# The experts' second product turned around: v stationary, the tokens' weights moving, the sum kept as features by tokens

## The chip, the cores and the metric

One Trainium2 chip, one NeuronCore of it. The metric is the device time of one execution of the whole program in microseconds (us). Everything is float32 at the inputs and the output; inside, most matrix products run on pairs of rounded float32 values (type fp32r), a high part and a rest, so that one exact product is three matmuls.

## The reference, cut to what matters

The program is two transformer blocks one behind the other on 256 tokens of 1024 features. The change touches only the last step of each of the two layers of the second block, a feed-forward part with 16,384 experts of which every token takes 128:

```
q = xn @ wq;  scores against 2 x 128 subkeys;  top 16 x 16;  idx, g = 128 experts and gates of each token
act = gelu(einsum('ckd,cd->ck', u_tab[idx], xn))
out = einsum('ck,ckd->cd', g * act, v_tab[idx])          # c token, k picked expert, d feature
x = x + out
```

The kernel doesn't gather the picked experts. It computes the product of every token with every expert's row of u (16,384 x 1024), multiplies it by a gate that is zero where the expert was not picked, and multiplies that with the whole of v (16,384 x 1024). The second of these products, weights (256 tokens x 16,384) times v, is what the change turns around.

## The kernel before, in words

The state x lives in SBUF as hT, features on the partitions (8 chunks of 128), tokens along the free dimension. The experts are worked off in 128 tiles t of 128 experts each (class Experts). A tile of u or v is one transfer of 512 KB. It lands in one of four slots of a ring (raw), is taken as two halves of 128 x 512, and each half is rounded by ScalarE into w_hi (line 214), while VectorE makes the rest w_lo (line 223). TensorE takes a half when its w_lo is made, and frees it with the last matmul that reads it; ScalarE may then round a later half into the same buffer. Four such buffers are in turn.

For the first 33 tiles (EARLY) the products with u were done ahead, so that the loop over t begins with 33 rounds that hold nothing but the product with v. In the other 95 tiles each round holds, on TensorE's queue, first the product of tile t + 1 with u (function product, lines 608 to 610: a 128 x 128 piece of the ring is stationary, 256 tokens move, 24 matmuls), and then the product of tile t with v (function add_up, lines 2088 to 2090). Beside that runs a chain between the two: ScalarE takes the gelu of the product out of PSUM (line 2103), VectorE multiplies by the gates (2130), ScalarE rounds the result (wt_hi, 2119), and VectorE makes its rest (wt_lo, 2146). It has a whole round of time.

In add_up the weights of 128 tokens are stationary and a half of v, 512 columns, moves: two groups of tokens, two halves, three matmuls each, so 12 matmuls of 512 columns, into four PSUM banks (acc) that sum over all 128 tiles, tokens on the partitions. At the end of a layer that sum stands the wrong way round for hT. So the four banks are copied to SBUF (VectorE line 2136, ScalarE 2109), turned by 16 TensorE transposes in eight groups (line 2074) into two PSUM banks in turn, and VectorE adds each group of features to hT (line 2140, eight times). The last of these additions releases the next layer, or the transfer of the output.

All queues are written in the order in which their engine executes them; nothing reorders the program.

Of the kernel before, what the change touches and what calls it, by code (L numbers as in the profile page):

```python
# [10 lines left out]
ACT = mybir.ActivationFunctionType  # L11
ALU = mybir.AluOpType
AX = mybir.AxisListType

P = 128
D = 1024
DC = D // P
LAT = 256
CTX = 256
# [12 lines left out]
NKEY = 128  # L32
# [16 lines left out]
class Span:  # L49


    def __init__(self, sem, first):
        self.sem, self.first = sem, first
# [112 lines left out]
def flat(ap):  # L166
    return ap.rearrange("p a b -> p (a b)")
# [1858 lines left out]
class Experts:  # L2026


    def __init__(self, k, l, x_hi, x_lo, early, gates, start):
        self.k, self.l, self.x_hi, self.x_lo, self.early, self.gates = k, l, x_hi, x_lo, early, gates  # L2030
        self.start = start
        self.ge = k.sb("ge", [P, 2, LAT], 151040)
        self.wt_hi = k.sb("wt_hi", [P, 2, LAT], 153088, F32R)
        self.wt_lo = k.sb("wt_lo", [P, 2, LAT], 155136, F32R)
        self.scores = {t: k.bank[t % 2].use(written=0) for t in range(EARLY, NKEY)}
        self.acc = [k.bank[2 + n].use(written=0) for n in range(4)]
        self.gated = k.named("scores_gated").take(NKEY - EARLY)
        self.hi = k.named("weights_t_rounded").take(NKEY)
        self.lo = k.named("weights_t_rest").take(NKEY)
        self.rowbuf = flat(gates[:, 0:8, :])  # L2040
        self.turns = [k.bank[n % 2].use() for n in range(DC)]
        self.done = [u.emptied() for u in self.turns[-2:]]

    def load(self, kind, t):
        self.k.ring.load(self.k.io[f"{kind}{self.l}"][t], (kind, self.l, t))
# [13 lines left out]
    def tensor(self):  # L2059
        k, pe = self.k, self.k.nc.tensor  # L2060
        for t in range(NKEY):
            if EARLY <= t + 1 < NKEY:
                use = self.scores[t + 1]
                pe.wait_ge(*use.free())
                product(k, use.tensor, [DC], lambda c: (self.x_hi[:, c, :], self.x_lo[:, c, :]), LAT)
            self.add_up(t)
        for n in range(DC):
            use = self.turns[n]
            if n == 0:
                for a in self.acc:  # L2070
                    pe.wait_ge(*a.emptied())
            pe.wait_ge(*use.free())
            for tt in range(2):
                m = pe.transpose(use.tensor[:, tt * P:(tt + 1) * P], self.rowbuf[:, tt * D + n * P:tt * D + (n + 1) * P],
                                 k.ident)
            m.then_inc(use.written.sem, 1)

    def add_up(self, t):
        k, pe, s = self.k, self.k.nc.tensor, t % 2
        pe.wait_ge(*self.lo.after(t + 1))  # L2080
        if t == 0:
            for a in self.acc:
                pe.wait_ge(*a.free())
        for half in range(2):
            hi, lo = k.ring.take()
            for tt in range(2):
                rows, out = slice(tt * P, (tt + 1) * P), self.acc[2 * tt + half].tensor[:]
                pe.matmul(out, self.wt_hi[:, s, rows], hi, start=(t == 0), stop=False, skip_group_check=True)  # L2088
                pe.matmul(out, self.wt_hi[:, s, rows], lo, start=False, stop=False, skip_group_check=True)  # L2089
                m = pe.matmul(out, self.wt_lo[:, s, rows], hi, start=False, stop=(t == NKEY - 1),  # L2090
                              skip_group_check=True)
            k.ring.free(m)

    def scalar(self):
        k, act = self.k, self.k.nc.scalar
        hold(act, self.start)
        self.round_weights(0)
        for t in range(NKEY):
            if EARLY <= t + 1 < NKEY:
                k.ring.round(2)  # L2100
                use = self.scores[t + 1]
                act.wait_ge(*k.ring.freed_of(("u", self.l, t + 1)))
                act.activation(self.ge[:, (t + 1) % 2, :], use.tensor[:, 0:LAT], ACT.Gelu).then_inc(use.read.sem, 1)
            if t + 1 < NKEY:
                self.round_weights(t + 1)
            k.ring.round(2)
        act.wait_ge(*k.ring.freed_of(("v", self.l, NKEY - 1)))
        for n in (1, 3):
            act.activation(self.rowbuf[:, n * 512:(n + 1) * 512], self.acc[n].tensor[:],
                           ACT.Copy).then_inc(self.acc[n].read.sem, 1)  # L2110

    def round_weights(self, t):
        act, s = self.k.nc.scalar, t % 2
# [7 lines left out]
    def vector(self):  # L2121
        k, dve = self.k, self.k.nc.vector
# [9 lines left out]
                self.weights_rest(t + 1)  # L2132
            k.ring.remain(2)
        dve.wait_ge(*k.ring.freed_of(("v", self.l, NKEY - 1)))
        for n in (0, 2):
            dve.tensor_copy(self.rowbuf[:, n * 512:(n + 1) * 512], self.acc[n].tensor[:]).then_inc(self.acc[n].read.sem, 1)
        for n, use in enumerate(self.turns):
            x = k.hT[:, n, CTX:]
            dve.wait_ge(*use.full())
            dve.tensor_tensor(x, x, use.tensor[:, 0:LAT], ALU.add).then_inc(use.read.sem, 1)  # L2140

    def weights_rest(self, t):
        dve, s = self.k.nc.vector, t % 2
# [301 lines left out]
```

## Time and profile before

| | us |
|---|---|
| Runs shown, median (lowest to highest of 3) | 3836.66 (3831.36 to 11778.27) |
| The profiled execution, its own time | 3843.8 |
| Its span in the profile | 3842.5 |
| Mean granted TensorE clock, share of 2.4 GHz | 0.923 |
| The experts' stage of the first layer, first to last matmul with v | 1986.5 to 2620.7 |
| The same of the second layer | 3199.0 to 3832.0 |
| From there to the issue of the output's transfer | 3832.0 to 3837.7 |

One of the three runs took 11778.27 us, far from the others; the median is not moved by it. Of the page, the busy line says how much of the span an engine had an instruction in progress, and the chain of waits says which instructions the end of the program depended on. For TensorE two rows of instructions are listed: PE, the matmuls, and PEld, the loads of the stationary operand. Their listed durations reach from issue to the drained result and overlap each other. What a matmul costs in a stream is the distance from its start to the next one's start, and that is what the rows below are for.

### The profile page before, as it was taken

How to read it: one execution, taken by the hardware profiler on the slowest of the kernel's cores; microseconds unless marked ns; L12 is line 12 of the kernel's file. 1: busy time of each engine (PE TensorE's matmuls, PEld its weight loads, DVE VectorE, ACT ScalarE, POOL GpSimd, SP SyncE). 2: the span in 40 equal slices, each digit the busy share in tenths (PEclk: the TensorE clock that was granted, in tenths of full speed). 3: DMA queues.
4: the chain of work that ended last, by engine and by line, in shares of the span. 5: the costliest groups of instructions: out<-in, count | busy, mean ns of one | idle time of the engine just before them, and what ended most of it. 6: DMA issues, size and time to landing. Idle time of an engine off the chain costs nothing.

```text
span 3842.5 us, 51118 instructions
## 1 busy us (share of the span) xinstructions
PE 3449.5 (90%) x19132; PEld 2853.0 (74%) x19132; DVE 2288.9 (60%) x4729; ACT 1810.7 (47%) x3796; POOL 0.2 (0%) x4
## 2 busy tenths in 40 slices
PE   7899889999979989589779999998869968999999
PEld 2474447887748988388668999997659857899998
DVE  6633334333465645768876666665665986666665
ACT  6622333332344534252585555554334196555554
POOL 0000000000000000000000000000000000000000
PEclk9897888999889989589999999998769999999999
DMA  8820001223203543044115555553204403555554
GB/s 310 286 99 11 1 23 66 99 90 94 94 5 110 179 139 122 0 138 143 66 53 184 186 187 187 186 186 128 72 26 161 160 1 125 186 186 186 186 186 154
DMA packets 134925, 479.90 MB, mean 125 GB/s; under 512 B 15384, under 2 KB 17304, under 8 KB 133912
## 3 DMA queue, kind: packets, MB, share of 16 engines
q1 hardware_dynamic: 130352, 463.53, 36.1%
q10 hardware_dynamic: 4328, 13.11, 0.9%
q8 instruction: 154, 2.52, 0.3%
q14 instruction: 91, 0.75, 0.1%
HBM read 475.53 MB, written 1.05 MB: 124 GB/s over the span
## 4 chain that ended last, share of the span: by engine, by line
PE 83%; DVE 9%; issue 3%; DMA 3%; ACT 3%; ACTq 0%; DVEq 0%
PE bank L608 14%; PE bank L610 13%; PE bank L609 13%; PE bank L2089 6%; PE bank L2088 6%; PE bank L2090 6%; PE bank L2014 6%; PE bank L1938 4%; PE bank L475 3%; PE bank L882 3%; DMA raw<-in_mod_w 2%; DVE conv L1313 1%; PE bank L484 1%; PE bank L892 1%; PE bank L1119 1%
## 5 line engine op out<-in xcount | busy, mean ns | idle before, releaser
L223 DVE TENSOR_TENSOR w_lo<-raw,w_hi 128x512 fp32r<-128x512 f32 x1664 | 1124.5, 691 | 798.3 <-ACT w_hi L214 769.0
L214 ACT ACTIVATE w_hi<-raw 128x512 fp32r<-128x512 f32 x1664 | 1011.9, 626 | 814.3 <-PE bank L610 606.6
L608 PE MATMUL bank<-x_hi,w_hi 128*128 128x256 f32 x2096 | 597.5, 285 | 14.9 <-DVE w_lo L223 7.3
L609 PE MATMUL bank<-x_lo,w_hi 128*128 128x256 f32 x2096 | 595.5, 284 | 0.0
L610 PE MATMUL bank<-x_hi,w_lo 128*128 128x256 f32 x2096 | 593.4, 283 | 0.0
L608 PEld LDWEIGHTS bank<-x_hi,w_hi 128*128 128x128 f32 x2096 | 398.1, 190 | 26.4 <-issue 8.2
L2088 PE MATMUL bank<-w_hi,wt_hi 128*128 128x512 f32 x1024 | 406.2, 397 | 6.5 <-DVE wt_lo L2146 6.5
L2089 PE MATMUL bank<-w_lo,wt_hi 128*128 128x512 f32 x1024 | 407.5, 398 | 0.0
L2090 PE MATMUL bank<-w_hi,wt_lo 128*128 128x512 f32 x1024 | 405.8, 396 | 0.0
L609 PEld LDWEIGHTS bank<-x_lo,w_hi 128*128 128x128 f32 x2096 | 398.2, 190 | 8.0
L610 PEld LDWEIGHTS bank<-x_hi,w_lo 128*128 128x128 f32 x2096 | 399.9, 191 | 0.0
L608 PE MATMUL bank<-a_hi,w_hi 128*128 128x512 f32 (+1 forms) x880 | 309.1, 351 | 18.0 <-DVE a_lo L580 18.0
L610 PE MATMUL bank<-a_hi,w_lo 128*128 128x512 f32 (+1 forms) x880 | 303.9, 345 | 0.0
L609 PE MATMUL bank<-a_lo,w_hi 128*128 128x512 f32 (+1 forms) x880 | 302.0, 343 | 0.0
L2014 PE MATMUL bank<-xn,u_raw 128*128 128x256 f32 x1056 | 228.2, 379 | 0.0
L2088 PEld LDWEIGHTS bank<-w_hi,wt_hi 128*128 128x128 f32 x1024 | 193.5, 189 | 45.9 <-DVE wt_lo L2146 6.9
L2090 PEld LDWEIGHTS bank<-w_hi,wt_lo 128*128 128x128 f32 x1024 | 193.2, 189 | 46.2
L1938 PE MATMUL bank<-hT,first 128*128 128x128 f32 x1024 | 147.5, 289 | 83.1 <-issue 77.2
L2089 PEld LDWEIGHTS bank<-w_lo,wt_hi 128*128 128x128 f32 x1024 | 193.8, 189 | 38.0
L2014 PEld LDWEIGHTS bank<-xn,u_raw 128*128 128x128 f32 x1056 | 200.5, 190 | 27.2
L1938 PEld LDWEIGHTS bank<-hT,first 128*128 128x128 f32 x1024 | 127.0, 195 | 103.7 <-issue 97.4
L608 PEld LDWEIGHTS bank<-a_hi,w_hi 128*128 128x128 f32 x880 | 167.6, 190 | 47.3 <-issue 13.9
(318 smaller groups left out, 4947.5 us busy)
## 6 DMA issues: line engine op xcount, KB each, us to landing
raw<-in_v SPq DMA_DIRECT2D x256, 512.0 KB, 4.4
raw<-in_u SPq DMA_DIRECT2D x190, 512.0 KB, 3.5
raw<-in_mod_w SPq DMA_DIRECT2D x96, 512.0 KB, 4.8
raw<-in_w_gate_up SPq DMA_DIRECT2D x88, 512.0 KB, 3.5
u_raw<-in_u SPq DMA_DIRECT2D x66, 512.0 KB, 3.5
raw<-in_w_in SPq DMA_DIRECT2D x40, 512.0 KB, 4.0
raw<-in_w_down SPq DMA_DIRECT2D x32, 512.0 KB, 3.5
raw<-in_w_peer SPq DMA_DIRECT2D x32, 512.0 KB, 3.9
```

Of the source, the lines that this page charges most:

```text
L214: self.nc.scalar.activation(self.hi[:, m % 4, :], self.half(m), ACT.Copy).then_inc(self.rounded[m % 4], 1)
L223: self.nc.vector.tensor_tensor(self.lo[:, m % 4, :], self.half(m), self.hi[:, m % 4, :], ALU.subtract).then_inc(self.ready[m % 4], 1)
L475: m = pe.matmul(self.sums.tensor[:, 4 * at:4 * at + P // group], k.sq[:, n % 4, t * P:(t + 1) * P], indicators[group], start=(n == 0 and t ...
L608: pe.matmul(out[:, 0:width], hi[:, w], x_hi, start=(c == 0), stop=False)
L609: pe.matmul(out[:, 0:width], hi[:, w], x_lo, start=False, stop=False)
L610: mm = pe.matmul(out[:, 0:width], lo[:, w], x_hi, start=False, stop=(c == total - 1))
L882: m = pe.matmul(use.tensor[:, 0:self.keys[r]], l, x, start=(j == 0), stop=(j == len(pairs) - 1))
L1938: m = pe.matmul(use.tensor[:, t * P:(t + 1) * P], self.first[:, g % 4, t, :], self.rows(g, t), start=True, stop=True)
L2014: m = pe.matmul(use.tensor[:, 0:LAT], self.raw[:, t % 3, c * P:(c + 1) * P], self.xn[:, c, :], start=(c == 0), stop=(c == DC - 1))
L2088: pe.matmul(out, self.wt_hi[:, s, rows], hi, start=(t == 0), stop=False, skip_group_check=True)
L2089: pe.matmul(out, self.wt_hi[:, s, rows], lo, start=False, stop=False, skip_group_check=True)
L2090: m = pe.matmul(out, self.wt_lo[:, s, rows], hi, start=False, stop=(t == NKEY - 1), skip_group_check=True)
```

## The change

The product with v is written the other way round. A 128 x 128 piece of the ring's half of v is stationary, and all 256 tokens' weights of the tile move. There are eight such pieces in a tile (four in each half) and three matmuls for each, so 24 matmuls of 256 columns take the place of 12 of 512. Each writes half a PSUM bank; the same four banks hold the sum, now features on the partitions and tokens along the free dimension, two chunks of features in a bank. The sum then stands as hT does: the copies to SBUF and the transposes are gone, and VectorE adds each bank to two chunks of hT in one instruction.

```
-        self.rowbuf = flat(gates[:, 0:8, :])
-        self.turns = [k.bank[n % 2].use() for n in range(DC)]
-        self.done = [u.emptied() for u in self.turns[-2:]]
+        self.done = [a.emptied() for a in self.acc]
...
             self.add_up(t)
-        for n in range(DC):
-            use = self.turns[n]
-            if n == 0:
-                for a in self.acc:
-                    pe.wait_ge(*a.emptied())
-            pe.wait_ge(*use.free())
-            for tt in range(2):
-                m = pe.transpose(use.tensor[:, tt * P:(tt + 1) * P], self.rowbuf[:, tt * D + n * P:tt * D + (n + 1) * P],
-                                 k.ident)
-            m.then_inc(use.written.sem, 1)
...
+        last = t == NKEY - 1
         for half in range(2):
             hi, lo = k.ring.take()
-            for tt in range(2):
-                rows, out = slice(tt * P, (tt + 1) * P), self.acc[2 * tt + half].tensor[:]
-                pe.matmul(out, self.wt_hi[:, s, rows], hi, start=(t == 0), stop=False, skip_group_check=True)
-                pe.matmul(out, self.wt_hi[:, s, rows], lo, start=False, stop=False, skip_group_check=True)
-                m = pe.matmul(out, self.wt_lo[:, s, rows], hi, start=False, stop=(t == NKEY - 1),
-                              skip_group_check=True)
+            for j in range(4):
+                c, cols = 4 * half + j, slice(j * P, (j + 1) * P)
+                out = self.acc[c // 2].tensor[:, (c % 2) * LAT:(c % 2 + 1) * LAT]
+                pe.matmul(out, hi[:, cols], self.wt_hi[:, s, :], start=(t == 0 and c % 2 == 0), stop=False,
+                          skip_group_check=True)
+                pe.matmul(out, hi[:, cols], self.wt_lo[:, s, :], start=False, stop=False, skip_group_check=True)
+                m = pe.matmul(out, lo[:, cols], self.wt_hi[:, s, :], start=False, stop=last, skip_group_check=True)
             k.ring.free(m)
...
-        act.wait_ge(*k.ring.freed_of(("v", self.l, NKEY - 1)))
-        for n in (1, 3):
-            act.activation(self.rowbuf[:, n * 512:(n + 1) * 512], self.acc[n].tensor[:],
-                           ACT.Copy).then_inc(self.acc[n].read.sem, 1)
...
         dve.wait_ge(*k.ring.freed_of(("v", self.l, NKEY - 1)))
-        for n in (0, 2):
-            dve.tensor_copy(self.rowbuf[:, n * 512:(n + 1) * 512], self.acc[n].tensor[:]).then_inc(self.acc[n].read.sem, 1)
-        for n, use in enumerate(self.turns):
-            x = k.hT[:, n, CTX:]
-            dve.wait_ge(*use.full())
-            dve.tensor_tensor(x, x, use.tensor[:, 0:LAT], ALU.add).then_inc(use.read.sem, 1)
+        for n, use in enumerate(self.acc):
+            x = k.hT[:, 2 * n:2 * n + 2, CTX:]
+            dve.tensor_tensor(x, x, use.tensor[:].rearrange("p (c t) -> p c t", c=2), ALU.add).then_inc(use.read.sem, 1)
```

The instructions move as follows. TensorE's queue at the end of the first layer's experts, before the change, ends with the sum, then the transposes, then the next layer's first norm (in these names wt is the tokens' weights, w the ring, and the number at a name counts the program's buffers):

```order
L2088 MATMUL bank<-w_hi_51,wt_hi_165 128x512
L2089 MATMUL bank<-w_lo_52,wt_hi_165 128x512
L2090 MATMUL bank<-w_hi_51,wt_lo_166 128x512
L2074 MATMUL bank<-cmat_54,gates_145 128x128 x16
L475 MATMUL bank<-ones_53,sq_57 128x1 x32
L484 MATMUL bank<-cmat_54,spread_58 128x128 x4
```

With the change the same place reads:

```order
L2078 MATMUL bank<-wt_hi_165,w_hi_51 128x256
L2080 MATMUL bank<-wt_lo_166,w_hi_51 128x256
L2081 MATMUL bank<-wt_hi_165,w_lo_52 128x256
L475 MATMUL bank<-ones_53,sq_57 128x1 x32
L484 MATMUL bank<-cmat_54,spread_58 128x128 x4
```

Three matmuls of 512 columns stood for a quarter of a tile, and now three of 256 stand for an eighth. The line of the 16 transposes is gone, and the next layer's norm follows the sum directly. VectorE's queue at the end of the program, as a difference:

```order
 L223 TENSOR_TENSOR w_lo_52<-raw_50,w_hi_51 128x512
-L2136 COPY gates_198<-bank 128x512 x2
-L2140 TENSOR_TENSOR hT_49<-hT_49,bank 128x256 x8
+L2123 TENSOR_TENSOR hT_49<-hT_49,bank 128x2x256 x4
```

Two copies and eight additions of 256 columns were there; four additions of 512 columns are there now, and nothing of TensorE stands between them. The transfers on SyncE's queue are the same, in the same order.

## Rows read from the trace of the kernel before

**Rows 1.** The page's busy line: busy us, share of the span, instructions.
```profile
PE 3449.5 (90%) x19132; PEld 2853.0 (74%) x19132; DVE 2288.9 (60%) x4729; ACT 1810.7 (47%) x3796; POOL 0.2 (0%) x4
```

**Rows 2.** The page's chain of waits, by line, as shares of the span.
```profile
PE bank L608 14%; PE bank L610 13%; PE bank L609 13%; PE bank L2089 6%; PE bank L2088 6%; PE bank L2090 6%; PE bank L2014 6%; PE bank L1938 4%; PE bank L475 3%; PE bank L882 3%; DMA raw<-in_mod_w 2%; DVE conv L1313 1%; PE bank L484 1%; PE bank L892 1%; PE bank L1119 1%
```

**Rows 3.** Busy times, clock and transfers of five stretches (us from the span's start).
```profile
core 0: us, PE busy (x) PEld busy (x) DVE busy (x) ACT busy (x) POOL busy (x), PEclk, DMA share, GB/s
1700.00:1740.00 40.00, 40.00 (x336) 40.00 (x335) 19.93 (x31) 20.94 (x40) 0.00 (x0) 1.00 0.64 218
1995.00:2075.00 80.00, 80.00 (x343) 64.34 (x342) 51.49 (x86) 44.67 (x85) 0.00 (x0) 1.00 0.55 187
2100.00:2600.00 500.00, 500.00 (x3171) 452.08 (x3170) 310.76 (x530) 274.22 (x530) 0.00 (x0) 1.00 0.56 186
2653.00:2656.00 3.00, 2.86 (x12) 2.81 (x12) 3.00 (x9) 1.76 (x5) 0.00 (x0) 0.50 0.03 5
2657.00:2661.00 4.00, 2.97 (x21) 2.36 (x19) 4.00 (x13) 2.40 (x6) 0.00 (x0) 1.00 0.00 0
```

**Rows 4.** Timeline of one round: start, us, engine, line; product with v begins at 2302.53.
```profile
2302.53 0.39 PE L2088 MATMUL bank<-w_hi,wt_hi 128*128 128x512 f32 x1
2302.54 0.19 PEld L2089 LDWEIGHTS bank<-w_lo,wt_hi 128*128 128x128 f32 x1
2302.76 0.40 PE L2089 MATMUL bank<-w_lo,wt_hi 128*128 128x512 f32 x1
2303.00 0.39 PE L2090 MATMUL bank<-w_hi,wt_lo 128*128 128x512 f32 x1
...
2305.33 0.28 PE L608 MATMUL bank<-x_hi,w_hi 128*128 128x256 f32 x1
2305.34 0.19 PEld L609 LDWEIGHTS bank<-x_lo,w_hi 128*128 128x128 f32 x1
2305.45 0.28 PE L609 MATMUL bank<-x_lo,w_hi 128*128 128x256 f32 x1
2305.57 0.28 PE L610 MATMUL bank<-x_hi,w_lo 128*128 128x256 f32 x1
...
2308.22 0.39 PE L2088 MATMUL bank<-w_hi,wt_hi 128*128 128x512 f32 x1
```

**Rows 5.** One line's instructions in all the program: the loads before L609's matmuls.
```profile
L609 PEld LDWEIGHTS bank<-x_lo,w_hi x2096: 187/188/338, 1441.4 to 3825.8; 128*128 128x128 f32 x191
```

**Rows 6.** The chain of waits in order of time, at the early products with u.
```profile
1749.64 113.98 PE bank L2014 x528
```

**Rows 7.** Timeline of the last end: from the last matmul to the output's transfer.
```profile
3831.57 0.39 PE L2090 MATMUL bank<-w_hi,wt_lo 128*128 128x512 f32 x1
3831.99 1.29 DVE L2136 COPY gates<-bank 128x512 f32<-128x512 f32 x2 [3.07 <-PE bank L2090]
3833.50 0.63 PE L2074 MATMUL bank<-cmat,gates 128*128 128x128 f32 x4 [1.54 <-DVE gates L2136]
...
3836.80 0.75 DVE L2140 TENSOR_TENSOR hT<-hT,bank 128x256 f32<-128x256 f32 x2 [0.20 <-PE bank L2074]
3837.65 0.63 SPq L2255 DMA_DIRECT2D out<-hT  x1
```

**Rows 8.** By line, shapes apart: a VectorE operation on 512 columns of PSUM and SBUF.
```profile
L1417 DVE TENSOR_TENSOR hid<-gate,bank 128x512 f32<-128x512 f32 x22 | 15.2, 689 | 30.5 <-PE bank L610 30.5
```

**Rows 9.** Timeline behind the first layer's end: copies, last additions, the next layer's start.
```profile
2620.74 1.29 DVE L2136 COPY gates<-bank 128x512 f32<-128x512 f32 x2
...
2625.55 0.75 DVE L2140 TENSOR_TENSOR hT<-hT,bank 128x256 f32<-128x256 f32 x2 [0.20 <-PE bank L2074]
2626.39 0.33 ACTq L256 DMA_DIRECT2D memT<-in_memT  x1
...
2634.61 13.79 PE L475 MATMUL bank<-ones,sq 128*128 128x1 f32 x64 [8.76 <-ACT sq L435]
```

**Rows 10.** Timeline of the ring in that round: ScalarE rounds, VectorE makes the rest.
```profile
2303.93 1.14 ACT L214 ACTIVATE w_hi<-raw 128x512 fp32r<-128x512 f32 x2
2304.06 0.42 DVE L2146 TENSOR_TENSOR wt_lo<-ge,wt_hi 128x256 fp32r<-128x256 f32 x1 [0.49 <-ACT wt_hi L2119]
2304.59 1.29 DVE L223 TENSOR_TENSOR w_lo<-raw,w_hi 128x512 fp32r<-128x512 f32 x2
2305.59 0.63 ACT L214 ACTIVATE w_hi<-raw 128x512 fp32r<-128x512 f32 x1 [0.52 <-PE bank L2090]
2306.26 0.69 DVE L223 TENSOR_TENSOR w_lo<-raw,w_hi 128x512 fp32r<-128x512 f32 x1 [0.38 <-ACT w_hi L214]
```

## The prediction

> **What bounds the kernel now.** I read the page's busy line first. TensorE has a matmul in progress for 90% of the span and no other engine comes near [rows 1]. That alone proves little, as such durations overlap, so the chain of waits comes next: the lines of the two expert products and their likes (608 to 610, 2088 to 2090) are most of it [rows 2]. Lines 2088 to 2090 are 18% of the span, some 690 us, and these are what the change rewrites. Then I asked for the experts' stage as stretches. In the part with both products, the stretch from 2100 to 2600, TensorE is busy for 500.00 of 500 us at a granted clock of 1.00 (the level of 2.4 GHz), VectorE for 311, ScalarE for 274, the transfers for 56% [rows 3]. In the part with v alone, from 1995 to 2075, it is 80.00 of 80 us [rows 3]. So the stage is paced by TensorE's stream without a gap, and a nanosecond more or less per matmul reaches the end in full. What a matmul costs is then the distance of starts in the timeline [rows 4].
>
> **The stream.** Removed: 12 matmuls of 512 columns in each of 128 tiles and two layers, 3,072. Added: 24 of 256 columns, 6,144. The columns are the same, 6,144 a tile. The old price: from 2302.53 to 2305.33 twelve matmuls take 2.80 us, 0.2333 each [rows 4]; in the part with v alone a window of 80 us holds 343 records, one or two of them begun before it, so 0.234 each, 2.81 us for twelve [rows 3]. The new price stands in the same round: lines 608 to 610 have exactly the new form, a piece of the ring stationary, 256 columns of tokens moving, three matmuls for a piece, and from 2305.33 to 2308.22 the 24 of them take 2.89 us [rows 4]. Over the 500 us the mean comes out a hair lower: 3,168 starts are 88 rounds of 5.68 us, less 2.80 is 2.88, 0.120 each. I take 2.88. Then each of the 95 rounds with both products costs 0.08 us more, each of the 33 with v alone 0.07, in two layers: 190 x 0.08 + 66 x 0.07 = **+19.8 us**.
>
> Each of the new matmuls brings its load of the stationary operand, so that 12 more loads a tile are to be hidden. A load is listed with 188 ns [rows 5], longer than the 120 ns between matmuls, yet the load for line 609 begins at 2305.34, just behind the start of line 608's matmul, and line 609's matmul follows at 2305.45 [rows 4]. Loads run beside the matmuls and beside each other. Until now the 512-column matmuls left them slack (452 of 500 us busy). A stretch without any is 1700 to 1740, the projection of the queries: loads busy 40.00 of 40 us and 336 matmuls, 0.120 each [rows 3]. A full load side therefore doesn't slow the stream beyond the 0.120 that I charge.
>
> Here a rule can be weighed. Between the price of a 512 and of two 256 the rows show 2 x 0.120 - 0.2333 = 6.7 ns. The Trainium skill (TensorE: Matmul & The Clock Gate, Back-to-back issue gap) gives the distance as columns over 2.4 GHz plus about 2.5 ns, so splitting a matmul costs 2.5 ns: its stream term would be +7.7 us in place of +19.8, the time 3838, which is counted with the first of the rivals. Its 216 ns for 512 columns is not what these rows show (233), so I take the rows.
>
> **The ring.** A half is consumed in 1.44 us where it was 1.40, and freed by its last matmul as before. ScalarE's rounding and VectorE's rest take 0.63 and 0.69 [rows 10], and each engine is idle for over a third of the stage [rows 3], so both keep up, more easily than before since the round is longer. The transfers (186 GB/s) have also more time. The gelu chain ends, with wt_lo at 2304.48 [rows 10], before the round's product with u even begins at 2305.33, and is needed at 2308.22: 3.7 us of slack. None of these costs or gains anything. While the clock is granted at 0.50 the columns cost twice as much either way; a split of equal columns changes nothing there.
>
> **The end of a layer.** Before: copies at 3831.99, the last pair of additions done at 3836.80 + 0.75 = 3837.55, 5.56 us [rows 7]; in the first layer 2620.74 to 2626.30, 5.56 as well [rows 9]. Now four additions of 512 columns follow the last matmul. The row nearest to them is a VectorE operation on 512 columns of PSUM and SBUF, 689 ns [rows 8]; two in a row take 1.29, not 1.38 [rows 7], so four take 0.69 + 3 x 0.60 = 2.5 to 4 x 0.69 = 2.8 us. With 2.6, each layer saves 3.0: **-6 us**. Nothing covers this tail: in the first layer ScalarE's transfers for the next mixer wait for it and are issued at 2626.39, and the next matmul comes 8.76 us after the last transpose [rows 9]; all that moves up. ScalarE's two copies were beside VectorE's and give nothing of their own. Without the transposes TensorE idles 11 to 12 us there instead of 8.8. It is at half clock anyway when it resumes and stays there: 2653 to 2656 has 0.50, 2657 to 2661 1.00 [rows 3]. The moment at which full clock returns may shift against the work by some us, which is worth at most 2 us here and at the like places behind it; I keep that as +-4 in the range and zero in the sum.
>
> **The sum.** +19.8 - 6.0 = +14 us. The profiled execution's own 3843.8 becomes 3858. It lies 7 us above the median of the runs shown; against that median, 3836.7, the forecast is **3851 us**, 0.4% slower. About 2% (77 us) is what a measurement of this kernel can tell from no change, so the forecast is "the same".
>
> **The rivals.**
>
> *The split is free.* If a moving operand that ScalarE and VectorE are just writing (the ring) is what makes 512 columns cost 0.2333, the old form paid for it and the new one, whose moving operand is quiet, does not. For it: line 2014, plain matmuls that move xn, takes 113.98 / 528 = 0.216 [rows 6] for the same 256 tokens in its type, less than 0.2333 for twice 256. Against it: line 608 moves quiet x as well and still pays 0.120. With 2 x 0.1167 the sum is -6: 3831. With 0.108 for each, half of line 2014's, it is 24 x 0.108 = 2.59 a tile, -0.21 x 256 - 6 = -60: 3777, 1.6% faster. Chances: 0.09 for the first, 0.03 for the second. That the queue keeps a stationary piece for two matmuls and drops a load would land here too; line 609 reuses line 608's piece today and has 2,096 loads of its own [rows 5].
>
> *The loads come out from behind the matmuls.* Place: add_up, where until now 512-column matmuls let the load side run ahead; with rounds of 48 short ones it can't. If the stream fell to one load at a time, 188 ns [rows 5], it would be 6,144 x (0.188 - 0.1167) = +438 us, 4270; it decides from 0.1167 + 77 / 6,144 = 0.129 us a matmul on, where the time is 2% up. Against it stands the stretch with the loads busy 40.00 of 40 us at 0.120 [rows 3]. The Trainium skill (the same page, The mechanism, in the part on packing small matmuls) says that a load overlaps a matmul in flight only when it goes to other rows of the array, which these full loads never do. By that rule nothing would overlap and this rival would hold; the trace disagrees, 0.11 to 0.12 us between starts with loads of 0.19 [rows 4]. Chance 0.03.
>
> *A little of it.* The new stream differs from line 608's in that it goes round four banks in half-bank pieces and that there is no other kind of matmul between. If it costs 0.123 to 0.129 that is +18 to +55 on the forecast, 3869 to 3906. Nothing in the rows asks for it. Chance 0.05.
>
> **How the numbers follow.** The forecast has the remaining 0.80. Its own spread: 1.5 ns on the price of a new matmul is 9 us, the clock 4, the tails 1, and two executions shown differ by 12; together about 3836 to 3868. The range takes in the free split at 3831 and the foot of the last rival: 3832 to 3871. Faster by over 2% would need more than the second free case: 0.01. Slower by over 2%: the loads and the far end of the last rival, 0.05. Within: 0.94.
>
> **What would show it.** Right: lines 2078 to 2081 with 6,144 matmuls of 256 columns; rounds of 5.76 us in the part with both products and 2.88 in the part with v alone; PEld busy near 100% of a stretch of 500 us; the experts' stages about 10 us longer each; from the last matmul to the output's issue 2.7 us instead of 5.7. Wrong: a distance of starts in add_up under 0.118 or over 0.123, a gap of TensorE behind line 223, or DVE and ACT suddenly waiting for something other than TensorE. What would overturn it most simply is a price of a moving column that depends on which buffer moves.

## The result and the profile after

The changed kernel takes 3849.43 us (median of 11 runs, 3845.79 to 3855.45), the kernel before 3836.11 (11 runs). The ratio is 1.0036 with a 95% interval of 1.0027 to 1.0044: 13.8 us slower, 10 to 17 by the interval. That is clear of noise and far inside 2%. (A difference with an interval is here, and below, the ratio of the runs times the time of the kernel before; the two medians alone differ by 13.3.) The forecast was 3851 and +14.

The two profiled executions differ by less, 3848.3 - 3842.5 = 5.8 us of span, and it takes the traces to see why. They can be laid side by side at four marks: the first and last matmul with v in each layer's experts' stage. These rows are from the timeline of the kernel before (start, us, engine, line; its last mark stands in [rows 7]):

```profile
1986.53 0.50 PE L2088 MATMUL bank<-w_hi,wt_hi 128*128 128x512 f32 x1 [3.27 <-DVE wt_lo L2146]
...
2620.31 0.40 PE L2090 MATMUL bank<-w_hi,wt_lo 128*128 128x512 f32 x1
...
3198.40 0.50 PE L2088 MATMUL bank<-w_hi,wt_hi 128*128 128x512 f32 x1 [3.27 <-DVE wt_lo L2146]
```

And these are from that of the changed kernel:

```profile
1977.66 0.58 PE L2078 MATMUL bank<-wt_hi,w_hi 128*128 128x256 f32 x1 [3.27 <-DVE wt_lo L2129]
...
2622.07 0.27 PE L2081 MATMUL bank<-wt_hi,w_lo 128*128 128x256 f32 x1
2622.38 2.48 DVE L2123 TENSOR_TENSOR hT<-hT,bank 128x512 f32<-128x512 f32 x4
2624.97 0.33 ACTq L256 DMA_DIRECT2D memT<-in_memT  x1
...
3196.86 0.38 PE L2078 MATMUL bank<-wt_hi,w_hi 128*128 128x256 f32 x1 [3.27 <-DVE wt_lo L2129]
...
3840.57 0.28 PE L2081 MATMUL bank<-wt_hi,w_lo 128*128 128x256 f32 x1
3840.89 2.48 DVE L2123 TENSOR_TENSOR hT<-hT,bank 128x512 f32<-128x512 f32 x4 [3.22 <-PE bank L2081]
3843.47 0.63 SPq L2238 DMA_DIRECT2D out<-hT  x1
```

| From start to start of the marks, us | before | after | difference |
|---|---|---|---|
| Start to the first stage (code that is not changed) | 1986.53 | 1977.66 | -8.9 |
| First stage | 633.8 | 644.4 | +10.6 |
| To the second stage, with the first layer's end | 578.1 | 574.8 | -3.3 |
| Second stage | 633.2 | 643.7 | +10.5 |
| Last matmul to the output's issue | 6.08 | 2.90 | -3.2 |

(The second stage of before begins with a matmul at 3198.40; the 3199.0 of the table ahead is half a microsecond late, and its other late marks are the ends of the last matmuls, 0.4 us behind their starts.) So in this pair of profiles the change costs 21.2 us in the stream and gives back 6.5 at the two ends. The 8.9 us in the first row lie in code that both kernels share, and hide more than half of it in this pair of profiles. Most of them arise around the first attention, where the one execution was granted its full clock earlier. One stretch of before and the same of after, columns as in [rows 3] (the second kernel is 2 us further on in its work where the stretch begins):

```profile
345.00:372.00 27.00, 27.00 (x56) 12.00 (x55) 7.82 (x20) 9.21 (x24) 0.00 (x0) 0.54 0.00 1
```

```profile
345.00:372.00 27.00, 26.91 (x80) 12.48 (x80) 10.51 (x28) 12.48 (x35) 0.00 (x0) 0.89 0.00 1
```

At a mean granted clock of 0.54 TensorE gets through 56 records, at 0.89 through 80, in code that is the same. In eleven profiles of this work the first stage begins between 1969.9 and 1986.5 us, the kernel before being the latest of all. A pair of profiles cannot weigh 14 us in this kernel; stage lengths can, they repeat within 1.2 us for one stream.

The stream itself, in the stretches that answer to [rows 3] (v alone, then both products):

```profile
1995.00:2075.00 80.00, 80.00 (x669) 80.00 (x669) 50.15 (x83) 43.23 (x82) 0.00 (x0) 1.00 0.54 184
2100.00:2600.00 500.00, 500.00 (x4169) 500.00 (x4169) 306.81 (x521) 269.77 (x521) 0.00 (x0) 1.00 0.56 183
```

TensorE is busy throughout as before, and now its loads are too, 500.00 of 500 us where they were 452. One or two records were begun before the window, so 4,167 matmuls in 500 us are 0.1200 each, and a round of 48 is 5.76 us. In the timeline the order is as regular as line 608's was; the second column is again each one's own duration, the distance of starts is the price:

```profile
2305.15 0.29 PE L609 MATMUL bank<-x_lo,w_hi 128*128 128x256 f32 x1
2305.27 0.28 PE L610 MATMUL bank<-x_hi,w_lo 128*128 128x256 f32 x1
2305.39 0.28 PE L2078 MATMUL bank<-wt_hi,w_hi 128*128 128x256 f32 x1
2305.51 0.28 PE L2080 MATMUL bank<-wt_lo,w_hi 128*128 128x256 f32 x1
2305.63 0.28 PE L2081 MATMUL bank<-wt_hi,w_lo 128*128 128x256 f32 x1
...
2308.27 0.28 PE L608 MATMUL bank<-x_hi,w_hi 128*128 128x256 f32 x1
```

From 2305.39 to 2308.27, 24 matmuls take 2.88 us; the twelve of before took 2.80 [rows 4].

### The profile page after: what moved, and what is told of

Its sections match the earlier page's. It is cut to its first block, busy times and chain, and to the rows that moved or that the text cites. A ratio compares the mean times of both kernels' runs of the same rounds, so it can differ in the third digit from the quotient of the medians.

```text
span 3848.3 us, 57182 instructions
## 1 busy us (share of the span) xinstructions
PE 3455.4 (90%) x22172; PEld 3007.1 (78%) x22172; DVE 2284.3 (59%) x4717; ACT 1807.5 (47%) x3792; POOL 0.2 (0%) x4
## 4 chain that ended last, share of the span: by engine, by line
PE 82%; DVE 9%; issue 3%; DMA 3%; ACT 3%; ACTq 0%; DVEq 0%
PE bank L608 14%; PE bank L609 13%; PE bank L610 13%; PE bank L2078 6%; PE bank L2080 6%; PE bank L2081 6%; PE bank L2014 6%; PE bank L1938 4%; PE bank L475 3%; DMA raw<-in_mod_w 2%; PE bank L882 2%; DVE conv L1313 1%; PE bank L484 1%; PE bank L892 1%; DVE stats L931 1%
## 5 line engine op out<-in xcount | busy, mean ns | idle before, releaser
L608 PE MATMUL bank<-x_hi,w_hi 128*128 128x256 f32 x2096 | 598.0, 285 | 14.8 <-DVE w_lo L223 7.3
L609 PE MATMUL bank<-x_lo,w_hi 128*128 128x256 f32 x2096 | 596.3, 284 | 0.0
L2078 PE MATMUL bank<-wt_hi,w_hi 128*128 128x256 f32 x2048 | 578.7, 283 | 6.5 <-DVE wt_lo L2129 6.5
L2080 PE MATMUL bank<-wt_lo,w_hi 128*128 128x256 f32 x2048 | 580.8, 284 | 0.0
L2081 PE MATMUL bank<-wt_hi,w_lo 128*128 128x256 f32 x2048 | 578.1, 282 | 0.0
L609 PEld LDWEIGHTS bank<-x_lo,w_hi 128*128 128x128 f32 x2096 | 398.6, 190 | 0.0
L2078 PEld LDWEIGHTS bank<-wt_hi,w_hi 128*128 128x128 f32 x2048 | 387.8, 189 | 6.9 <-DVE wt_lo L2129 6.9
L2081 PEld LDWEIGHTS bank<-wt_hi,w_lo 128*128 128x128 f32 x2048 | 389.1, 190 | 0.0
L2080 PEld LDWEIGHTS bank<-wt_lo,w_hi 128*128 128x128 f32 x2048 | 385.5, 188 | 0.0
L609 PE MATMUL bank<-a_lo,w_hi 128*128 128x512 f32 (+1 forms) x880 | 305.9, 348 | 0.0
```

Source lines behind the costliest of these rows:

```text
L608: pe.matmul(out[:, 0:width], hi[:, w], x_hi, start=(c == 0), stop=False)
L609: pe.matmul(out[:, 0:width], hi[:, w], x_lo, start=False, stop=False)
L2078: pe.matmul(out, hi[:, cols], self.wt_hi[:, s, :], start=(t == 0 and c % 2 == 0), stop=False, skip_group_check=True)
L2080: pe.matmul(out, hi[:, cols], self.wt_lo[:, s, :], start=False, stop=False, skip_group_check=True)
L2081: m = pe.matmul(out, lo[:, cols], self.wt_hi[:, s, :], start=False, stop=last, skip_group_check=True)
```

## The experiments

Nine kernels, to take the sum apart and then to price a matmul by itself.

### The split alone

```
-                pe.matmul(out, self.wt_hi[:, s, rows], hi, start=(t == 0), stop=False, skip_group_check=True)
+                for x in range(2):
+                    n = slice(x * 256, (x + 1) * 256)
+                    pe.matmul(out[:, n], self.wt_hi[:, s, rows], hi[:, n], start=(t == 0 and x == 0), stop=False,
+                              skip_group_check=True)
```

(and the two matmuls behind it in the same way.)

> The kernel before with its 512-column matmuls of the v product each cut in two of 256 columns: the weights stay stationary, the ring still moves, the old end of a layer stays. It is the stream half of the change alone, without turning the operands. My theory (a matmul of 256 columns of these pairs has one price, about 0.120 us, whichever operand moves, and two of them cost 6 to 7 ns more than one of 512): the distance of starts in the v product is 0.120, each experts' stage 10.6 us longer than 633.5, 3836 + 21 = 3857 us in all. Rival (the moving ring, which is being written, costs extra per column, and the change escaped a part of that): the distance is clearly above 0.120, 0.123 or more, 3875 us or more. Rival (a repeated stationary operand makes its second load cheap): under 0.118, 3845 us or less.

Measured: 3846.29 us, ratio 1.0024 (1.0013 to 1.0035) to the kernel before, which took 3834.76 beside these runs: +9.2 us with 5 to 13 by the interval. The two stages are 639.5 and 640.2 us, 12.8 more than before in all. Both are under my 21. The distance of starts in the v product is 0.1188, under my 0.120 and over the 0.118 of the rival with the cheap second load, so neither theory has it:

```profile
2100.00:2600.00 500.00, 500.00 (x4194) 500.00 (x4192) 308.06 (x523) 271.57 (x524) 0.00 (x0) 1.00 0.57 185
```

4,194 records against the changed kernel's 4,169, with the same 48 matmuls a round, and the half of these that are lines 608 to 610 lie at 0.120 in both. So splitting costs 2 x 0.1188 - 0.2335 = 4 ns a pair, about 13 us, and turning the operands another 1.2 ns a matmul, 7.4 us. By the stages turning costs 8.4 us (1288.1 against 1279.7); the last microsecond lies in lines 608 to 610, 0.2 ns each.

### The end of a layer alone

```
-        for n in (0, 2):
-            dve.tensor_copy(self.rowbuf[:, n * 512:(n + 1) * 512], self.acc[n].tensor[:]).then_inc(self.acc[n].read.sem, 1)
-        for n, use in enumerate(self.turns):
...
+        for n, use in enumerate(self.acc):
+            x = k.hT[:, 2 * n:2 * n + 2, CTX:]
+            dve.tensor_tensor(x, x, use.tensor[:].rearrange("p (c t) -> p c t", c=2), ALU.add).then_inc(use.read.sem, 1)
```

> The kernel before with only the end of a layer changed: the copies and transposes are left out and the four accumulators, which still hold tokens by features, are added to the state as they stand, so the values are not the reference's. It is the other half of the change alone. My theory: from the start of the last matmul to the output's issue 2.9 us in place of 6.1, 3.2 us less at each of two layers, 3836 - 6.4 = 3830 us. Rival (the next layer's start is held by something else, such as its transfers or the clock's return, so that only the last layer gains): 3833 us. If both halves are additive, this one and the split sum up to the changed kernel's +13 us.

Measured: 3829.79 us, ratio 0.998 (0.9967 to 0.9993), 7.7 us less, 3 to 13 by the interval. The stages stay (1267.1 us in all, before 1266.9). The timeline's end:

```profile
3830.33 0.39 PE L2078 MATMUL bank<-w_hi,wt_lo 128*128 128x512 f32 x1
3830.76 2.48 DVE L2121 TENSOR_TENSOR hT<-hT,bank 128x512 f32<-128x512 f32 x4 [3.07 <-PE bank L2078]
3833.33 0.63 SPq L2236 DMA_DIRECT2D out<-hT  x1
```

3.00 us from the last matmul to the output's issue, 6.08 before; 3.1 less. The first layer's end is as short here and in the changed kernel, where it is 2622.07 to 2624.97, 2.90 us. But the rival (only the last layer gains, for the clock's return) is not refuted: its 3833 lies inside the interval, and in this very profile the second stage begins 578.7 us after the end of the first, not earlier than before (578.1). The next mixer does start earlier; what it gained is lost within 130 us of the first stage's end. These are the same 652 matmuls, from the mixer's first one of line 608 on, in the kernel before, the changed kernel and this one:

```profile
2653.90:2750.20 96.30, 87.18 (x652) 85.39 (x651) 52.18 (x99) 45.24 (x92) 0.00 (x0) 0.91 0.37 122
```

```profile
2652.30:2748.60 96.30, 87.18 (x652) 85.44 (x652) 52.23 (x99) 45.25 (x92) 0.00 (x0) 0.91 0.38 122
```

```profile
2649.90:2749.00 99.10, 90.71 (x652) 89.32 (x652) 52.24 (x99) 45.25 (x92) 0.00 (x0) 0.86 0.38 118
```

At a mean granted clock of 0.86 instead of 0.91 they take 2.8 us more. Of the eight profiles with the short end, four have 574.8 to 576.2 us between the stages and four 577.9 to 578.7; the two with the old end have 578.1 and 578.5. So the last layer's 3.1 us reach the end in each of them, the first layer's only where the clock doesn't take them back. Averaged over runs more than the one end comes through: the changed kernel is 13.8 us slower (10 to 17) with 21.2 us in its stages, which leaves 7.4 (4 to 11) for the ends. With both ends in full the halves add up: 12.8 + 8.4 - 6.4 = +14.8, measured +13.8.

### Turned, but 512 columns wide

```
+            twice = [wt[:, s, :].unsqueeze(1).to_broadcast([P, 2, LAT]) for wt in (self.wt_hi, self.wt_lo)]
+            for j in range(2):
+                cols = slice(2 * j * P, (2 * j + 1) * P)
+                out = self.acc[2 * half + j].tensor[:].rearrange("p (c t) -> p c t", c=2)
+                pe.matmul(out, hi[:, cols], twice[0], start=(t == 0), stop=False, skip_group_check=True)
```

> The changed kernel, but with only every second piece of v as the stationary operand (half the features are left out) and the tokens' weights moving twice in one matmul of 512 columns: 12 matmuls of 512 columns a tile, with the operands in the new places. Same columns as before and after. My theory (the price goes by the width alone): the distance of starts is 0.2335 as before the change, the stages 633.5 us, the end of a layer short: 3836 - 6.4 = 3830 us. Rival (a quiet moving operand streams faster than the ring): 0.216 to 0.230, that is 3775 to 3820 us.

Measured: 3832.52 us, ratio 0.9989 (0.9976 to 1.0002). The stages are 633.4 and 634.1 us, 1267.5 in all, and the stretch has the counts of [rows 3] to the record:

```profile
2100.00:2600.00 500.00, 500.00 (x3171) 451.81 (x3171) 310.88 (x529) 273.63 (x528) 0.00 (x0) 1.00 0.59 186
```

At 512 columns it makes no difference whether the ring or the weights move: 0.2335 either way. The rival of the quiet operand falls. What the change lost it lost by the width, and in the 256-column form alone the turned placing costs something too. (Between the stages this profile has 578.0 us, one of the four in which the first end's gain is lost again; by the runs it is 4 us less than before, 9 less to 1 more, where I expected 6.4 less.)

### The prices with nothing else running

```
+        for _ in range(96):
+            pe.matmul(out[:, 0:512], wt[:, 0:128], hi, start=True, stop=True)
+        for _ in range(96):
+            pe.matmul(out[:, 0:384], wt[:, 0:128], hi[:, 0:384], start=True, stop=True)
+        for _ in range(96):
+            pe.matmul(out[:, 0:256], wt[:, 0:128], hi[:, 0:256], start=True, stop=True)
+        for _ in range(96):
+            pe.matmul(out[:, 0:256], hi[:, 0:128], wt, start=True, stop=True)
...
```

> The changed kernel with eight segments of 96 matmuls of the same pairs behind the last layer, when ScalarE, VectorE and the ring's transfers stand still: 512, 384 and 256 columns with the weights' buffer stationary (128 wide); 256 with the ring's piece stationary; the last with a stationary operand of 64 columns, and 512 with one of 64; then 96 in the exact order and banks of the changed product and 96 in the order of the old one cut in two. They write sums that are read by nobody. Theory A (the pair type itself costs 0.444 ns a column plus a fixed 6 ns): at full clock 0.2335, 0.177 and 0.1195 to 0.120 even when nothing else runs, and 64-wide loads change nothing. Theory B (the 8% over 0.4167 ns a column is the traffic of ScalarE, VectorE and the transfers): 0.216, 0.163 and 0.109. Theory C (the load of 128 columns is what makes 256 columns cost 0.119 instead of 0.117): the 64-wide segment of 256 columns is at 0.117 or less while the 512 ones are alike. For the 1.2 ns between the turned order (120.0) and the cut old order (118.85): if it comes from the operands themselves, the last two segments show it too; if from the ring being rewritten, they are equal.

The chain of waits in order of time merges each segment: start, us, count. The first runs partly at half clock.

```profile
3850.19 24.05 PE bank L2260 x96
3874.24 16.65 PE bank L2262 x96
3890.89 11.39 PE bank L2264 x96
3902.28 11.51 PE bank L2266 x96
3913.80 11.23 PE bank L2268 x96
3925.02 21.78 PE bank L2270 x96
```

Divided: 384 columns 0.1734; 256 with the weights stationary 0.1186; 256 turned 0.1199; 256 turned with 64-wide loads 0.1170; 512 with 64-wide loads 0.2269. The full-clock part of the first is 0.2343 each. The last two segments, in the order of the changed product and of the split one, come to 0.1200 and 0.1187. Theory B falls clearly: with VectorE, ScalarE and the transfers silent every price is what it was in the stage. The 1.2 ns of turning are there as well (1.3 here), so they are not the ring being rewritten. Theory A holds for 512 and 256, misses 384 by 4 ns (0.177 expected), and was wrong on the loads: a 64-wide one makes 256 columns 3 ns cheaper, as theory C has it, but also 512 columns by 7 ns, where theory C expected no change and where the load side is idle for 40% of the time (11.33 of 19 us busy from 3926 to 3945). A 64-wide stationary piece also writes 64 partitions of the sum instead of 128; no run tells that from the shorter load.

### Half-wide loads in the real stream

```
-                c, cols = 4 * half + j, slice(j * P, (j + 1) * P)
+                c, cols = 4 * half + j, slice(j * P, j * P + 64)
```

> The changed kernel with 64 of the 128 columns of each stationary piece (half of the features are left out), so that each load is half as long while the 24 matmuls of 256 columns a tile stay. Theory A (the price of a matmul is its columns plus a fixed part, loads are hidden in full): 0.120 as before, experts' stages 644 us, 3849 us. Theory C (the load side, busy for 500 of 500 us, holds the stream back a little): the distance falls to 0.117 or less in the v product while lines 608 to 610 stay at 0.120, the stages 635 us or shorter, 3830 us.

Measured: 3827.32 us in one run, stages 638.6 and 633.5 us, against 644.4 and 643.7. The distance in the v product fell to 0.1183 in the first layer and to 0.1167 in the second, while lines 608 to 610 stayed at 0.120. Two stretches, one of each layer:

```profile
2100.00:2600.00 500.00, 500.00 (x4198) 500.00 (x4197) 308.82 (x526) 272.12 (x526) 0.00 (x0) 1.00 0.57 185
3300.00:3800.00 500.00, 500.00 (x4228) 500.00 (x4227) 311.00 (x529) 273.61 (x528) 0.00 (x0) 1.00 0.58 186
```

Theory C is right in direction, and in the second layer in size: a stationary piece of half the width makes the stream of 256 columns a little faster. That it is the load that holds it back is argued, not shown, for the reason given above. Why the same code runs at two prices in two layers stays open.

### The three matmuls in another order

```
-                pe.matmul(out, hi[:, cols], self.wt_lo[:, s, :], start=False, stop=False, skip_group_check=True)
-                m = pe.matmul(out, lo[:, cols], self.wt_hi[:, s, :], start=False, stop=last, skip_group_check=True)
+                pe.matmul(out, lo[:, cols], self.wt_hi[:, s, :], start=False, stop=False, skip_group_check=True)
+                m = pe.matmul(out, hi[:, cols], self.wt_lo[:, s, :], start=False, stop=last, skip_group_check=True)
```

> The changed kernel with the second and third matmul of each piece exchanged: high part times high weights, rest times high weights, high part times rest of the weights. Now the moving operand repeats behind itself where the stationary one did. If the 1.2 ns by which the turned product lies over the cut old one (118.85) depends on a stationary operand repeating, the distance changes (below 119.5 or above 120.5, the stage by 4 us or more); if it depends on which buffer is stationary, it stays 120.0 and the stage 644 us.

Measured: 3850.54 us in one run, both stages 643.7, and the same 4,169 matmuls in the stretch as in the changed kernel:

```profile
2100.00:2600.00 500.00, 500.00 (x4169) 500.00 (x4168) 306.70 (x521) 270.12 (x521) 0.00 (x0) 1.00 0.56 183
```

A repeated stationary operand brings nothing and costs nothing.

### Which buffer is stationary, which moves

Thirteen segments as in the quiet experiment, all 256 columns and 128-wide loads, and three of other widths:

```
+        for _ in range(64):
+            m = pe.matmul(out[:, 0:256], x[:, 0:128], hi[:, 0:256], start=True, stop=True)
+        for _ in range(64):
+            m = pe.matmul(out[:, 0:256], hi[:, 0:128], x[:, 0:256], start=True, stop=True)
...
```

> The changed kernel with sixteen segments of 64 matmuls behind the last layer, nothing else running: 256 columns with a 128-wide stationary operand in thirteen pairs of buffers (weights, rest of weights, two ring buffers, the ring's rest, two chunks of x), then a stationary operand of 32 columns with 256, then 512 and 320 columns. They write sums that nobody reads. Theory A (which buffer is stationary and which moves has its own price, by where the two lie in SBUF): weights stationary and ring moving 118.7 ns, the turned pair 120.0, and other pairs fall on these two or more levels by their places. Theory B (it is not the place, and the 1.3 ns between the segments before was their order in time): all thirteen within 0.4 ns. For the load: 32 columns stationary at 116.9 as 64 were if 116.7 is the floor of the moving side, lower if the load still counts. Widths: 320 at 0.148 to 0.149 and 512 at 0.233 if a fixed part of 6 ns stands beside 0.444 ns a column.

Four rows of the chain: weights stationary and ring moving, the turned pair, x stationary and ring moving, 320 columns.

```profile
3851.35 7.51 PE bank L2263 x64
3858.86 7.68 PE bank L2265 x64
3897.25 7.59 PE bank L2275 x64
3973.36 9.39 PE bank L2293 x64
```

0.1173, 0.1200, 0.1186 and 0.1467. Ten of the thirteen pairs lie at 0.120; only the three whose moving operand is the ring's buffer and whose stationary one is not come out lower, at 0.1173 to 0.1187. That looks like theory A, but the pair of weights and ring, 0.1186 in the quiet experiment, is 0.1173 here with the same instructions, so the place is not all of it. What makes the 1 to 3 ns is not settled. With a 32-wide load the same pair took 0.1178, no less than its 0.1173 with a 128-wide one: here a load of a quarter of the width brought nothing, which speaks against the load as the cause of these 1 to 3 ns.

### Where loads become the bound

```
+        for _ in range(80):
+            m = pe.matmul(out[0:128, 0:128], hi[:, 0:128], wh[:, 0:128], start=True, stop=True)
...
+        for _ in range(80):
+            m = pe.matmul(out[0:64, 0:128], hi[:, 0:64], wh[:, 0:128], start=True, stop=True)
...
```

> The changed kernel with ten segments of 80 matmuls of the pair type behind the last layer, nothing else running, the ring's buffer stationary and the weights' moving as in the changed product: 256, 224, 192, 128 and 64 moving columns with 128 stationary; 256, 224, 128 and 64 with 64 stationary; 256 with 96 stationary. Theory C (the 120 ns of the changed product lie just over a floor that loads of 128 columns set, so the split had used up nearly all that hides them): the distance stops falling soon under 256 columns, at 107 to 118 ns, and falls on only with 64 stationary. Theory A (loads are hidden with much to spare, the 2 to 3 ns are a small fixed cost): it falls in step with the columns, 105 at 224, 91 at 192, 62 at 128, alike for both widths. A third outcome: columns cost more under 256, so that the short ones are no cheaper than 120, with either width.

Again the chain, one row a segment: 256, 224, 192, 128 and 64 columns on 128-wide loads, 256, 224, 128 and 64 on 64-wide ones, 256 on a 96-wide one.

```profile
3856.64 9.60 PE bank L2263 x80
3866.24 8.93 PE bank L2265 x80
3875.17 8.92 PE bank L2267 x80
3884.09 8.90 PE bank L2269 x80
3892.99 13.45 PE bank L2271 x80
3906.43 11.26 PE bank L2273 x80
3917.69 8.26 PE bank L2275 x80
3925.95 4.80 PE bank L2277 x80
3930.76 4.64 PE bank L2279 x80
3935.39 9.47 PE bank L2281 x80
```

With 128-wide loads the price is 0.120 at 256 columns and then stands still, 0.1116, 0.1115 and 0.1113 at 224, 192 and 128. With 64-wide ones it goes on down, 0.1033 at 224 and 0.060 at 128, and stops at 0.058. This is theory C as written: the width of the stationary piece sets a floor, 0.1115 us for 128 and 0.058 for 64, and the 256 columns of the changed product stand only 8 ns above it. I call this floor the slot of one load. The Trainium skill (TensorE: Matmul & The Clock Gate, LDWEIGHTS) counts a load as its columns over 1.2 GHz, 107 ns for 128 and 53 for 64; the slots measured here are each about 5 ns more. Segments five and six can't be priced, since the clock dropped in them (below).

### The old stream with a shorter end

```
-        self.turns = [k.bank[n % 2].use() for n in range(DC)]
+        self.turns = [k.bank[b].use() for b in (0, 1, 6, 7)]
...
+        for g, use in enumerate(self.turns):
+            if g % 2 == 0:
+                for a in self.acc[g // 2::2]:
+                    pe.wait_ge(*a.emptied())
...
+            dve.tensor_tensor(x, x, use.tensor[:].rearrange("p (c t) -> p c t", c=2), ALU.add).then_inc(use.read.sem, 1)
```

> The kernel before with its 512-column stream and a shorter end of a layer: the transposes go in four groups of two chunks to four PSUM banks (none waits for an earlier addition), the first two groups start behind the first pair of copies, and VectorE makes four additions of 512 columns. My theory: 5.56 us from the first copy to the last addition become about 3.8, 1.8 less at each layer, 3836 - 3.5 = 3832 us, 17 us under the changed kernel. Rival (the end of a layer is bound by VectorE's own instructions, two copies and four additions of 0.6 to 0.69 us and the wait between them): 4.4 us, 3834 us.

Measured: 3831.62 us, ratio 0.999 (0.9979 to 1.0). The stages are 1266.9 us. The end of the program:

```profile
3820.76 0.39 PE L2092 MATMUL bank<-w_hi,wt_lo 128*128 128x512 f32 x1
3821.19 1.09 ACT L2111 ACTIVATE gates<-bank 128x512 f32<-128x512 f32 x2 [3.80 <-PE bank L2092]
3821.19 1.29 DVE L2138 COPY gates<-bank 128x512 f32<-128x512 f32 x2 [3.07 <-PE bank L2092]
3821.94 1.97 PE L2076 MATMUL bank<-cmat,gates 128*128 128x128 f32 x16 [0.79 <-DVE gates L2138]
3822.63 2.48 DVE L2142 TENSOR_TENSOR hT<-hT,bank 128x512 f32<-128x512 f32 x4 [0.15 <-PE bank L2076]
3825.20 0.63 SPq L2257 DMA_DIRECT2D out<-hT  x1
```

4.44 us where 6.08 stood, 1.6 less at each layer, 3.3 in all, as expected within 0.2 each. From the first copy to the last addition it is 3.9 us, near my 3.8 and not the rival's 4.4. The first layer's 1.6 us don't show between the stages, which are 578.4 us apart. VectorE is now busy from the first copy to the last addition with 0.15 us of waiting, so a shorter end would have to take work away from it. This version is 18 us under the changed kernel by the medians and 3 under the kernel before, the latter at the edge of what the interval tells.

## Why the prediction was right

**The bound.** Right. TensorE streams without a gap in both kernels, so the price of a matmul went through to the end in full.

**The stream, +19.8 us.** Right in size, 21.2 measured, since I took the price from lines 608 to 610, which have not only the width but also the placing of the new form (ring stationary, quiet operand moving). The step behind it, that two times 256 costs 6.7 ns more than 512, is a sum of two things I didn't separate: 4 ns for the split and 1.2 ns a matmul for the turned placing. A price from a 256-column matmul with the ring moving would have given +13. My simplest sign of being wrong, a price that depends on which buffer moves, did in fact turn up, only small: 0.1173 to 0.120 over thirteen pairs of buffers.

The Trainium skill's 2.5 ns for every further matmul (TensorE: Matmul & The Clock Gate, Back-to-back issue gap, which gives it for a matmul by itself, without a load for each) made +7.7 for the stream. The split by itself measured 12.8, nearer to it than to my 20, but still above.

**The loads.** Right at this width, by little. The sum held, with loads busy 500.00 of 500 us and no slower than 0.120. What I didn't see is how near the limit was: the slot of a load, 0.1115 us, is just under the price of 256 columns, and a stationary piece of half the width makes the same stream 2 to 3 ns faster. The rival in which loads come out from behind the matmuls did not happen, by a margin of 8 ns. It was right to read 1700 to 1740 [rows 3] as evidence against it, wrong to feel far from it. The Trainium skill's rule that would have made it true (same page, The mechanism), that a full load never overlaps a matmul in flight, doesn't hold in any of these rows; the same section also lets a load go ahead of the matmuls into a background buffer of weights, which I had left out.

**The free split.** It did not happen: at 512 columns the quiet operand costs the same 0.2335. One of its supports was misread. Line 2014 has 528 records in 113.98 us, but the kernel writes 33 x 8 = 264 matmuls there, two records each. So one plain float32 matmul of 256 columns takes 0.432 us, not 0.216, and the 0.108 that I made of it, with the 3777, had no ground. The forecast doesn't use it. (The other free case, 3831, also lies just outside the 3832 at which the range begins.)

**The end of a layer, -6 us.** Right in the pair of profiles, -6.5: four additions in 2.48 us where I said 2.6 (they begin 0.60 us apart, the last takes 0.68), in both layers. The next layer's start moved up with it: the transfers were issued 2.90 us after the last matmul's start, not 6.08. TensorE idled 10.65 us there instead of 8.76, a little less than the 11 to 12 I had. But "all that moves up" holds for the first layer only in part: in four of eight profiles with the short end the start of the second stage did not move, since code just behind the end ran at a lower granted clock. I had put that at 2 us at most here; it took 2.8 in the one shown.

**The ring, the transfers, the gelu chain, zero.** Right. In the stage VectorE and ScalarE waited only for TensorE and for each other, as before.

**The clock, zero within 4 us.** Too narrow for a pair of executions: shared code before the stage shifted by 9 us. Over 11 runs each it averages out: the median is within 2 us of the forecast, while single runs of the changed kernel lie up to 10 us apart.

## What to carry to other kernels

Turning a product so that its result stands right saves the transposes at the end, but here it halves the moving width in a loop that runs 256 times; multiply the difference of two distances of starts by the count before looking at the end. Take the new form's price from a row that has its width and its placing, and check how far the moving time lies above the slot of one load: with 128-wide loads 256 columns are near the edge (0.120 against 0.1115), and 128 columns would cost almost as much as 256. The end could be shortened here without touching the loop, 4.4 us for 6.1. And a few microseconds saved between two stages can be taken back by the clock of the code behind them: look for them at the next stage's start, in more than one execution.

## What the runs showed of the hardware that was not expected

A moving width under 256 columns brings almost nothing with 128-wide loads: 128 columns take 0.1113 us, 256 take 0.120. With 64-wide loads 128 columns take 0.060.

A plain float32 matmul of 256 columns takes 0.432 us (line 2014, 264 of them in 113.98 us [rows 6]), more than the three of a pair product with 0.120 each.

The granted clock fell in the middle of a stream without a gap. In the segment with 64 moving columns on 128-wide loads TensorE had an instruction in progress all the time, and yet this window of it has a clock of 0.63, as that segment began at the full 2.4 GHz and dropped to 1.2; the next one began at 1.2 and came back to 2.4 while 256 columns moved:

```profile
3894.00:3905.00 11.00, 11.00 (x66) 11.00 (x65) 0.00 (x0) 0.00 (x0) 0.00 (x0) 0.63 0.00 0
```

The segment before, with 128 moving columns on the same loads, and the two with 128 and 64 columns on 64-wide loads kept the full clock, but none of them lasted longer than 9 us. TensorE had no idle time in any of them.
